# Turning 128x128 blocks as two 64-row halves, each half of the array writing a PSUM bank of its own

## The reference, cut to what matters

```
# block 1
hn = rmsnorm(h)                      # 256 x 1024
proj = hn @ w_in                     # q, k, v of two attentions, gates
p  = softmax(q k^T * scale + c_t - c_s, causal)      # "fox", 8 heads, in 128-query blocks
y_fox = p @ v
q, k, v = silu(causal_conv4(gq, gk, gv));  q, k = l2norm(q), l2norm(k)
o = gated_delta_rule(q, k, v, g, beta)               # chunks of 64, 8 heads
o = rmsnorm(o) * silu(z)
h = h + (sigmoid(g1) * (y_fox @ w1) + sigmoid(g2) * (o @ w2)) @ w_out
h = h + (silu(gate) * val) @ w_down   # gate, val = conv3(rmsnorm(h) @ w_up)
# block 2
q, k, v, u = rmsnorm(rmsnorm(h)) @ w_in_2            # q, k normalised per head
h = h + concat(neighbourhood_attention(q, k, v), multiscale_pool(u)) @ w_out_2
h = h + (silu(hn @ w_gate) * (hn @ w_up)) @ w_down_2
```

## Time and profile before

| what | value |
|---|---|
| median of three runs | 818.33 us |
| time of the profiled execution | 817.55 us |
| its span, first to last instruction | 816.2 us |
| TensorE busy | 804.7 us, 99% |
| weight loads busy | 738.6 us, 90% |
| VectorE busy | 589.5 us, 72% |
| ScalarE busy | 446.9 us, 55% |
| mean granted TensorE clock | 1.000 |

### The profile page before, as it was taken

The page is one execution under the profiler, slowest core; times in us unless marked ns, Lnnn a source line. Parts: engine busy times, 40 slices in busy tenths (PEclk is TensorE's granted clock), DMA queues, the critical chain, the costliest instruction groups (busy, mean ns, idle before and its releaser), DMA issues.

```text
span 816.2 us, 14536 instructions
## 1 busy us (share of the span) xinstructions
PE 804.7 (99%) x5910; PEld 738.6 (90%) x5910; DVE 589.5 (72%) x967; ACT 446.9 (55%) x721; POOL 76.6 (9%) x67
## 2 busy tenths in 40 slices
PE   7999999999999999999999999999999999999998
PEld 5999999999999999899999998888777888888886
DVE  6878878785553746669999997486766777777543
ACT  5666577654454444455656563456664656555441
POOL 0001000001010401100211011012100111011000
PEclk9999999999999999999999999999999999999999
DMA  8754663646440564575687766555424666565541
GB/s 261 234 172 143 192 223 109 181 136 186 116 134 31 163 199 162 200 232 167 198 244 223 240 199 208 185 185 177 155 78 132 207 203 203 173 192 193 192 162 72
DMA packets 130194, 144.18 MB, mean 177 GB/s; under 512 B 11456, under 2 KB 110928, under 8 KB 129872
## 3 DMA queue, kind: packets, MB, share of 16 engines
q1 hardware_dynamic: 127680, 141.19, 54.6%
q10 hardware_dynamic: 2448, 2.05, 1.0%
HBM read 141.78 MB, written 1.46 MB: 175 GB/s over the span
## 4 chain that ended last, share of the span: by engine, by line
PE 94%; DVE 2%; DMA 1%; ACT 1%; issue 0%; POOL 0%; ACTq 0%; DVEq 0%; POOLq 0%
PE bank L551 92%; DVE panel_lo L1469 1%; DMA panel_raw<-in_w_in 1%; PE bank L597 1%; DMA h<-in_x 1%; PE bank L889 0%; PE bank L619 0%; ACT panel_hi L1019 0%; PE bank L839 0%; DVE blocks_T L1628 0%; DVE decayT L1532 0%; PE bank L862 0%; PE bank L674 0%; DVE x_halves L1490 0%; DVE blocks_X L1631 0%
## 5 line engine op out<-in xcount | busy, mean ns | idle before, releaser
L1469 DVE TENSOR_TENSOR panel_lo<-panel_raw,panel_hi 128x1024 fp32r<-128x1024 f32 x252 | 319.3, 1270 | 153.4 <-ACT panel_hi L1019 153.1
L551 PE MATMUL bank<-x_halves,panel_hi 128*128 128x256 f32 (+1 forms) x1952 | 415.3, 304 | 1.7 <-DVE x_halves L1490 1.5
L1019 ACT ACTIVATE panel_hi<-panel_raw 128x1024 fp32r<-128x1024 f32 x252 | 266.6, 1059 | 176.7 <-PE bank L551 171.4
L551 PEld LDWEIGHTS bank<-x_halves,panel_hi 128*128 128x128 f32 x1952 | 315.3, 191 | 17.1 <-DVE panel_lo L1469 1.7
L551 PE MATMUL bank<-x_halves,panel_lo 128*128 128x256 f32 x1152 | 324.8, 282 | 0.0
L551 PEld LDWEIGHTS bank<-x_halves,panel_lo 128*128 128x128 f32 x1152 | 219.8, 191 | 0.0
L551 PE MATMUL bank<-panel_hi,x_halves 128*128 128x256 f32 (+1 forms) x384 | 88.1, 324 | 0.0
L551 PEld LDWEIGHTS bank<-panel_hi,x_halves 128*128 128x128 f32 x384 | 63.4, 190 | 5.8 <-issue 0.7
L551 PE MATMUL bank<-panel_hi,act_hi 128*128 128x512 f32 x176 | 68.6, 390 | 0.0
L551 PE MATMUL bank<-panel_hi,act_lo 128*128 128x512 f32 x176 | 68.5, 389 | 0.0
L551 PE MATMUL bank<-panel_lo,act_hi 128*128 128x512 f32 x176 | 68.5, 389 | 0.0
(11 more groups left out here) (284 smaller groups left out, 973.3 us busy)
## 6 DMA issues: line engine op xcount, KB each, us to landing
panel_raw<-in_w_in SPq DMA_DIRECT2D x38, 1024.0 KB, 5.3
panel_raw<-in_w_up SPq DMA_DIRECT2D x30, 1024.0 KB, 5.3
panel_raw<-in_w_down SPq DMA_DIRECT2D x20, 1024.0 KB, 5.1
panel_raw<-in_w_gate SPq DMA_DIRECT2D x10, 1024.0 KB, 5.3
panel_raw<-in_w_out SPq DMA_DIRECT2D x8, 1024.0 KB, 5.1
panel_raw<-in_w_in SPq DMA_DIRECT2D x12, 512.0 KB, 4.6
panel_raw<-in_w_branch_fox SPq DMA_DIRECT2D x4, 1024.0 KB, 5.2
panel_raw<-in_w_branch_gdn SPq DMA_DIRECT2D x4, 1024.0 KB, 5.1
```

The source lines that it names most:

```text
L551: return e.matmul(o, l, r, start=start, stop=stop, skip_group_check=True)
L1019: return e.activation(o, i_, ACT.Copy, scale=scale)
L1469: e.tensor_tensor(lo, raw_view(i, k0, kt), hi.bitcast(F32), ALU.subtract).then_inc(s_lo, 1)
```

## The change

Except for the first eight blocks of the first norm, `na_turn`, `row_factor` and `x_turn2`, each 128x128 transposition becomes two of 64 rows: the upper 64 rows of the block against the upper 64x64 identity, and the lower 64 rows against the lower one. Each gives 64 of the 128 output columns. They are issued upper, lower, upper, lower, and the two kinds go to different banks. This is done in two ways:
- `turn_blocks` (conv_turn, fox_turn, qk_turn): all upper halves go to bank n, all lower halves to bank n + 1, n even; the key takes **both** banks, and the copy out reads both with a pattern of 64-column pieces. `room` waits for the last users of both banks.
- `turn_four` (turn_x but for the first half of "mix", and turn_units): four banks are filled together, so that each ends with whole blocks; in a first pass the upper half of block 0 and the lower half of block 1 and so on, then in a second pass the other halves. Before the second pass into a pair of banks TensorE waits for its own first pass there (`s_turned`).

`turn_x` now has a key and a bank per feature block, not per two. The diff, cut:

```diff
-        def bank_for(ring, key):
-            n = rings[ring][ring_at[ring] % len(rings[ring])]
-            ring_at[ring] += 1
+        def bank_for(ring, key, two=False):
+            at_ = ring_at[ring]
+            if two and rings[ring][at_ % len(rings[ring])] % 2:
+                at_ += 1
+            n = rings[ring][at_ % len(rings[ring])]
+            ring_at[ring] = at_ + 1 + two
             place[key] = (n, uses[n])
             uses[n] += 1
+            before[key] = []
+            for m in (n, n + 1)[:1 + two]:
+                if m in used_by and used_by[m] not in before[key]:
+                    before[key].append(used_by[m])
+                used_by[m] = key
             return banks[n]
...
         def room(key):
-            n, use = place[key]
-            return [(s_emptied[n], use)] if use else []
+            return [emptied(p) for p in before[key]]
...
+        def turned_blocks(key, n):
+            first = 512 * place[key][0]
+            return psum[:, first:first + 1024].rearrange("p (g u c) -> p u g c", g=2, c=64)[:, 0:n]
...
+            def turn_blocks(key, blocks):
+                for u, src in enumerate(blocks):
+                    for g, r in enumerate(BLOCKS_64):
+                        i_ = e.transpose(turned_blocks(key, len(blocks))[:, u, g, :], src[r, :], ident[r, r])
+                i_.then_inc(will_fill(key), 1)
...
+            def turn_four(keys, blocks):
+                for key in keys:
+                    side(key)
+                    for s, v in room(key):
+                        e.wait_ge(s, v)
+                for swap in range(2):
+                    for two in range(2):
+                        if swap:
+                            e.wait_ge(s_turned, halves_turned[0] - 1 + two)
+                        for u in range(len(blocks[0])):
+                            for i in range(2):
+                                b, r = 2 * two + i, BLOCKS_64[i ^ swap]
+                                o = bank_of(keys[b])[:, u * P:(u + 1) * P]
+                                i_ = e.transpose(o[:, r], blocks[b][u][r, :], ident[r, r])
+                                if swap and u == len(blocks[0]) - 1:
+                                    i_.then_inc(will_fill(keys[b]), 1)
+                        if not swap:
+                            i_.then_inc(s_turned, 1)
+                            halves_turned[0] += 1
...
             def fox_turn(hh):
                 key = ("fox_t", hh)
-                bank = bank_for("fox", key)
+                bank_for("fox", key, True)
                 for s, v in room(key):
                     e.wait_ge(s, v)
                 e.wait_ge(s_fox_norm, hh + 1)
-                for u in range(3):
-                    i_ = e.transpose(bank[:, u * P:(u + 1) * P], fox_p[hh % 3][:, u * P:(u + 1) * P], ident)
-                i_.then_inc(will_fill(key), 1)
+                turn_blocks(key, [fox_p[hh % 3][:, u * P:(u + 1) * P] for u in range(3)])
...
-                            for j in (2 * c, 2 * c + 1):
-                                turn_x(x, j)
+                            turn_half_x(x, c)
...
-                copy(fox_pT[hh % 2], bank_of(("fox_t", hh))[:, 0:3 * P]).then_inc(empties(("fox_t", hh)), 1)
+                copy(as_blocks(fox_pT[hh % 2]), turned_blocks(("fox_t", hh), 3)).then_inc(empties(("fox_t", hh)), 1)
```

More of the change, by code:

```diff
@@ L528, in x_ready @@
             if x in ("mix", "ffn", "norm1", "norm2"):
-                return emptied(("turn", x, j))
+                return emptied(("turn", x, 2 * j + 1))
             if x == "yf":
@@ new lines, in x_blocks @@
+            def x_blocks(f):
+                return [h[:, m, f * P:(f + 1) * P] for m in range(TT)]
+            def turn_x(x, j):
+                for f in (2 * j, 2 * j + 1):
+                    key = ("turn", x, f)
+                    bank = side(key)
+                    for s, v in room(key):
+                        e.wait_ge(s, v)
+                    for m, src in enumerate(x_blocks(f)):
+                        i_ = e.transpose(bank[:, m * P:(m + 1) * P], src, ident)
+                    i_.then_inc(will_fill(key), 1)
@@ L600, in row_factor, with turn_half_x @@
+            def turn_half_x(x, c):
+                features = range(4 * c, 4 * c + 4)
+                turn_four([("turn", x, f) for f in features], [x_blocks(f) for f in features])
             def row_factor(x, order):
@@ L616, in conv_turn @@
                 e.wait_ge(s_gated, c + 1)
[L617 to L620, removed]
+                turn_blocks(key, [src[:, f, t * P:(t + 1) * P] for f in range(2) for t in range(TT)])
             def q_sums(c):
@@ L855, in qk_turn @@
                 key = ("qk_turn", j, s_)
-                b3 = pairs(side(key))
+                bank_for("side", key, True)
                 for s, v in room(key):
@@ L859, in qk_turn @@
                 e.wait_ge(s_n_tok, j + 1)
[L860 to L863, removed]
+                turn_blocks(key, [qk2[:, j, m, s_, f * P:(f + 1) * P] for f in range(2) for m in range(TT)])
             def na_scores(pair):
@@ L939, in tensor_program @@
                 if n == 1:
[L940 to L943, removed]
+                    e.wait_ge(s_h_act, 2)
+                    e.wait_ge(s_h_dve, 6)
+                    turn_half_x("mix", 1)
                 if n in (15, 17, 25, 27):
@@ L1037, in turn_x @@
             def turn_x(x, j, gain):
[L1038 to L1042, removed]
+                for f in (2 * j, 2 * j + 1):
+                    e.wait_ge(*filled(("turn", x, f)))
+                    i_ = copy(xhi[:, f, :], bank_of(("turn", x, f))[:, 0:T], gain[:, f:f + 1])
                 i_.then_inc(s_xhi, 1)
@@ L1076, in conv_out @@
                 kind, j = CONVS[c]
-                bank = units(bank_of(("conv_turn", c)))
+                blocks = turned_blocks(("conv_turn", c), 4)
                 e.wait_ge(*filled(("conv_turn", c)))
                 if kind == "k":
-                    copy(tok_k[:, four_units(j), :], bank).then_inc(empties(("conv_turn", c)), 1)
+                    copy(as_blocks(tok_k[:, four_units(j), :].rearrange("p u d -> p (u d)")), blocks).then_inc(empties(("conv_turn", c)), 1)
                 else:
@@ L1083, in conv_out @@
                     for u in range(4):
-                        i_ = copy(tok_v[:, 4 * j + u, :], bank[:, u, :], inv_rk[:, 4 * j + u:4 * j + u + 1])
+                        i_ = copy(as_blocks(tok_v[:, 4 * j + u, :]), blocks[:, u:u + 1], inv_rk[:, 4 * j + u:4 * j + u + 1])
                     i_.then_inc(empties(("conv_turn", c)), 1)
@@ L1485, in turn_x @@
             def turn_x(x, j, gain, order):
-                b3 = pairs(bank_of(("turn", x, j)))
                 e.wait_ge(s_xhi, order)
[L1488 to L1492, removed]
+                for f in (2 * j, 2 * j + 1):
+                    e.scalar_tensor_tensor(xlo[:, f, :], bank_of(("turn", x, f))[:, 0:T], gain[:, f:f + 1],
+                                           xhi[:, f, :].bitcast(F32), ALU.mult, ALU.subtract) \
+                        .then_inc(empties(("turn", x, f)), 1)
             def conv_taps(c, backs):
```

34 lines of the change are left out of this document (11 added, 23 removed).

## The result

The changed kernel takes **832.76 us** (median of six, 828.5 to 833.7 but for one of 3082) against 817.99: ratio **1.0169**, 95% interval 1.0148 to 1.0191. The ratio leaves out that execution and the one of 1600 before the change; both medians count them. A second set of executions gave 1.0195 (1.0170 to 1.0220). The forecast was 830, range 822 to 838. So it is slower by 1.7 to 2%, 14 to 16 us.

The account below looks back on a forecast made before the run. TensorE, busy 99% of the span, was taken to bound the kernel. Fox stage +11.0, conv +1.1, x +0.8, yg -0.4 and q/k +0.3 sum to 12.8 us on 817.55: forecast 830 us, range 822 to 838.

Parts of the forecast that it names:

- Part 1: All changed turns: two 64-row halves overlap in the array, 0.062 us a pair where a whole block took 0.109.
- The rival at 838: All changed turns: halves or their loads don't overlap, a block costs 0.12 us, 8.4 us more in all; chance 0.16.
- Part 2: Turns outside the fox stage: entering and leaving the 64-row form costs 0.34 us per excursion; conv +1.1, x +0.8, yg -0.4, q/k +0.3.
- Part 3: Fox stage: turns need the next head's scores emptied by `fox_bias`, so TensorE waits; +11.0 us, bounds 7.5 and 14.
- Turns 0 and 1: Fox turns of heads 0 and 1: wait for `fox_bias`; turn 0 stalls 2.55 us, turn 1 starts at 174.25, 6.85 late.
- Values 1: `fox_values` of head 1, behind turn 1: start at 177.55 instead of 171.44, 6.1 us late.
- Turn 2: Fox turn of head 2: waits for `fox_bias(3)` behind a 7.2 us key bias DMA; starts 187.85, 9.25 us late.
- Turn 4: Fox turn of head 4: waits 1.18 us for VectorE, counted as 1.0.
- The rival of the clock: TensorE's clock falls in a fox stall, work takes up to 2.8 us longer, total 833 us; chance 0.07.
- No slower, 819.4: Fox stage: stalls don't come because `fox_bias` empties the scores in time, leaving only the +1.8 of Part 2; chance 0.07.

Follow-up runs that it names:

- experiment 1: Changed kernel with the fox turns put back to three whole 128x128 transpositions into one bank: 819.63 us, ratio 1.0022.
- experiment 2: Changed kernel with fox turns as whole transpositions into one bank, but the key still taking both banks: 831.75 us, ratio 1.0171.
- experiment 5: Changed kernel with fox turns of heads 0 to 2 in halves on two side banks, heads 3 to 7 whole in one bank: 821.12 us, ratio 1.0047.
- experiment 4: Changed kernel with 20 identity products on TensorE ahead of the wait of head 1's fox turn: 832.14 us, ratio 1.0179.
- experiment 7: Changed kernel with 18, 10 and 5 identity products ahead of the fox turns of heads 1, 2 and 4: 831.81 us; again 832.32 us.
- experiment 6: Changed kernel with only head 0's fox turn whole and in one bank: 833.89 us, ratio 1.0197.
- 9: Kernel before, with halves only in yg and the first q/k pair, and whole fox turns of heads 0 to 2 on side banks: 816.06 us, ratio 0.9969.

## Why the prediction was right, and where it wasn't

- **Part 1, halves side by side: right.** 0.0625 us a pair (0.11 from the first to the second) against 0.062. The Trainium skill's 107 ns for a load of 128 columns (TensorE: Matmul & The Clock Gate, LDWEIGHTS) isn't borne out for these transpositions: loads of 128 columns kept up with 0.0625 a pair. The rival at 838 is out.
- **Part 2, 0.34 us per excursion: right.** conv +0.13 (foreseen +0.15), x +0.09 (+0.11), yg -0.41 (-0.4), q/k -0.18 and +0.50 (-0.1 and +0.4), the last for the wait for ScalarE's copy as foreseen. Outside the fox stage 1.4 in all, foreseen 1.8.
- **Part 3, every turn issued before its second bank is free: right as a mechanism** (experiments 1, 2 and 5). Its sum, 11.0 for 12.26, came near because errors cancel. What follows counts by the yardstick, that is less the 0.62 us by which `fox_scores(1)` was late already.
  - Turns 0 and 1: foreseen at 159.62 and 174.25, measured at 159.51 and 174.02. VectorE's queue doesn't know that TensorE is already 0.62 late, and was a little early itself. Turn 1 is 6.0 late and not 6.85: 0.85 less.
  - Values 1: foreseen 6.1 late, measured 8.4 by the trace's time, 7.8 by the yardstick. **This is the step that failed**: the sum holds no cost for the clock, whose fall had a chance of 0.07. From turn 1 to values 1 are 5.8 us here and 3.3 where TensorE was kept busy (experiment 4): 2.5 us for the fall. Experiment 4's values 1 are only 2.1 earlier because its products outlast the wait by 0.35.
  - Turn 2: the forecast kept the DMA of 7.2 us, because the inverted blocks would move by as much as it. The clock's fall broke that: the blocks left 5.3 us later, the key bias 8.5. The transfer took 4.6, and VectorE took its result up 0.9 later than before. From values 1 to the end of `fox_bias(3)` are 8.66 us for 10.22: 1.55 less. So turn 2 was 9.99 late in the trace's time (9.4 by the yardstick), against 9.25: an error of 2.3 up and one of 1.55 down nearly cancel.
  - Turn 4: the wait foreseen with 1.18 was 1.17, but a second fall behind it cost 1.5: 7.16 us to values 4, where the same kernel run again, without a fall there, and experiment 7 have 5.6 to 5.7.
  - The stage of experiment 1 is 0.36 us shorter than before too, which the forecast didn't have.
  - Together 11.0 - 0.85 + 2.5 - 1.55 + 1.5 - 0.35 = 12.25.
- **The rival of the clock** was priced at 833 for one fall, and the median is 832.8. The price of one fall was near, 2.8 us for 2.5, and its chance far too small. That the total meets 833 is luck: there were two falls, and three errors the other way. "After the warm-up no wait of TensorE passes 1.75 us" should have been read the other way: the trace of before couldn't say what a wait of 4 us does, and the change was known to make one.
- **No slower, 819.4**: it is what experiment 1 shows when the second bank isn't asked for, 819.6.

## What to carry to other kernels

When a step is to take two buffers of a ring of two, list first who holds the second one, when it is released, and by which queue: here that cost nine times what the operations themselves did, and two idle banks of the other ring cost nothing (experiment 5). Give a new wait of some microseconds on TensorE the price of the clock too, and don't count on getting it back by keeping TensorE busy: in experiment 4 the next wait, which hung on another engine and a DMA, took it. A switch to half-array tiles costs about 0.3 us there and back here: 4 blocks lose 0.13 us, 8 lose 0.09 or gain 0.18, 16 gain 0.41.

## What the runs showed of the hardware

- The clock fell to 0.50 after an idle time of 4.0 us and stayed for about 6 us of full work. Behind waits of 1.2 to 1.7 us it fell in some executions and not in others: at turn 4 (1.17 us) in the changed kernel's first trace and not in its second; at turn 0 in its second (1.61) and not in its first (1.66); at turn 2 in experiment 6 (1.71) and not in experiment 2 (1.70).
- The key bias of head 3 took 6.7 to 7.3 us to land in the eight traces in which the inverted blocks left within 0.7 us of it, and 4.6 to 5.5 in the six others.
- The same products ran at two paces, 454 or 463 in 80 us, with a granted clock of 1.00 in both, one pace for the whole stage in each profiled execution: 2.3 us of a span.
- Traces of the changed kernel and of those made from it reach the fox stage up to 1.5 us apart, in two ways. In the changed kernel's second trace and in experiments 6 and 9 the clock fell near the start (0.67 to 0.71 from 10 to 14 us), after waits of 2.2 to 2.4 us for VectorE's `h`, which in the others are 0.9 to 1.9; `h` itself came no later. In both traces of experiment 7's kernel the clock stayed at 1.00, and TensorE waited 1.1 us for ScalarE's `conv_acc` at 25 us. With the paces this makes a comparison of two single profiles of this kernel uncertain by nearly 4 us, unless it is read stage by stage.
